# Scores of layer 0 in two rounded passes over stacked key halves, projections one PSUM bank at a time, joined latent weights

## The reference, cut to what matters

```python
qa, ka, va, f_logit, qb, kb, vb = jnp.split(h @ w_in, cuts, axis=-1)
# fox
s = jnp.einsum('bqhd,bkhd->bhqk', q, k) * (HEAD_DIM ** -0.5)
p = jax.nn.softmax(jnp.where(visible, s + decay, NEG_INF), axis=-1)
# stick-breaking
z = jnp.einsum('bqhd,bkhd->bhqk', q, k) * (HEAD_DIM ** -0.5)
later = lax.cumsum(log_rest, axis=-1, reverse=True) - log_rest
a = jnp.exp(log_beta + later)
# layer 1
z = h @ w_down                       # 384 + 256 + 32 columns
cq, ckv, kr = jnp.split(z, [Q_LORA, Q_LORA + KV_LORA], axis=-1)
```

## Time and profile before

| | |
|---|---|
| median of 3 runs | 1447.9 us (1446.54 to 1451.47) |
| the profiled execution's own time | 1455.13 us |
| its span, first to last instruction | 1453.4 us |
| PE, DVE, ACT busy | 1203.3, 655.4, 391.2 us |

### The profile page before, as it was taken

One profiled execution on the slowest core, in us unless ns is written; L12 is line 12 of the kernel. 1 busy time (PEld: TensorE's weight loads), 2 busy tenths in 40 slices (PEclk: granted clock), 3 DMA queues, 4 the chain that ended last, 5 costly groups with the idle time before them and its releaser, 6 DMA issues. The chain is left out here.

```text
span 1453.4 us, 23857 instructions
## 1 busy us (share of the span) xinstructions
PE 1203.3 (83%) x8148; PEld 833.9 (57%) x8148; DVE 655.4 (45%) x1819; ACT 391.2 (27%) x903; POOL 239.9 (17%) x366
## 2 busy tenths in 40 slices
PE   7999999987966997777497899999799499877760
PEld 5777777765854564344264676766587355444430
DVE  5455544446571542122362355555566445222227
ACT  4334444445111211011121244444521021111111
POOL 1222232220103232221110000000001222222113
PEclk9899999999977999999798999999899599989995
DMA  5222324206169999999620300000032999999965
GB/s 177 76 68 74 105 91 147 94 18 243 73 286 339 375 364 374 378 372 411 255 75 19 131 17 16 31 15 16 22 143 119 365 374 359 359 374 384 394 275 195
DMA packets 61407, 290.75 MB, mean 200 GB/s; under 512 B 12720, under 2 KB 23152, under 8 KB 44288
## 3 DMA queue, kind: packets, MB, share of 16 engines
q1 hardware_dynamic: 49440, 265.90, 49.5%
q0 software_dynamic: 10560, 18.90, 4.1%
q10 hardware_dynamic: 1312, 4.72, 0.8%
HBM read 275.91 MB, written 29.29 MB: 210 GB/s over the span
## 5 line engine op out<-in xcount | busy, mean ns | idle before, releaser
L1738 PE MATMUL psum<-w_gu,moe_xgT 128*64 128x256 f32 x1968 | 261.2, 410 | 71.1 <-DMA w_gu<-in_w_gate_up 56.1
L1738 PEld LDWEIGHTS psum<-w_gu,moe_xgT 128*64 128x64 f32 x1968 | 154.2, 146 | 162.3 <-issue 116.3
L199 PE MATMUL psum<-x_hi,ab_w_hi 128*128 128x288 f32 x384 | 126.6, 330 | 2.7 <-DVE ab_k_tok L877 1.6
L1811 DVE COPY moe_xgT<-psum 128x512 f32<-128x512 f32 x64 | 44.3, 692 | 166.0 <-PE psum L1728 165.1
L201 PE MATMUL psum<-x_hi,ab_w_lo 128*128 128x288 f32 x384 | 115.7, 301 | 0.0
L1685 POOL DMA_INDIRECT y_d<-mix,moe_slots x60 | 55.5, 926 | 364.0 <-DVE mix L1824 364.0
L200 PE MATMUL psum<-x_lo,ab_w_hi 128*128 128x288 f32 x384 | 115.6, 301 | 0.0
L1786 ACT ACTIVATE moe_silu<-psum 64x256 f32<-64x256 f32 x64 | 24.2, 378 | 338.9 <-PE psum L1738 293.8
L1755 PE MATMUL psum<-w_dn,moe_hidT 128*64 128x512 f32 x352 | 85.1, 604 | 2.2 <-issue 2.2
L1819 DVE COPY moe_hidT<-psum 128x128 f32<-128x128 f32 x64 | 18.7, 291 | 143.1 <-PE psum L1746 141.5
L199 PEld LDWEIGHTS psum<-x_hi,ab_w_hi 128*128 128x128 f32 x384 | 74.5, 194 | 9.5 <-issue 7.6
(11 more groups left out here) (305 smaller groups left out, 2124.0 us busy)
## 6 DMA issues: line engine op xcount, KB each, us to landing
w_gu<-in_w_gate_up SPq DMA_DIRECT2D x54, 2048.0 KB, 35.4
w_dn<-in_w_down SPq DMA_DIRECT2D x44, 1024.0 KB, 37.4
xT<-in_w_down SPq DMA_DIRECT2D x20, 1024.0 KB, 38.6
w_gu<-in_w_gate_up SPq DMA_DIRECT2D x10, 1536.0 KB, 40.5
w_gu<-in_w_out SPq DMA_DIRECT2D x4, 2048.0 KB, 7.9
combine_ys<-y_d SPq DMA_DIRECT2D x16, 512.0 KB, 8.5
xT<-in_w_gate_up SPq DMA_DIRECT2D x10, 512.0 KB, 41.8
xT<-cum_d SPq DMA_DIRECT2D x8, 544.0 KB, 6.6
```

Source lines behind the costliest of these rows:

```text
L199: nc.tensor.matmul(dst, r32(ah), r32(bh), start=first, stop=False)
L1738: last = nc.tensor.matmul(gu(s)[h * CB:(h + 1) * CB, 0:EH], xgT[:, s, j, :], gate_up_tile(k.w_gu[n], j)[:, h * EH:(h + 1) * EH], start=(j ...
L1811: nc.vector.tensor_copy(xgT[:, s, :, :].rearrange("p j q -> p (j q)"), xtr(s)).then_inc(xgT_ready, 1)
```

## The change

- Scores of layer 0: two fp32r passes in place of one fp32 product. `k_both` holds for each head the rounded keys on one half of the partitions and their low rest on the other; `q_hi` holds the rounded queries on both halves (the second by a copy), `q_lo` their rest on one half and zeros on the other. The first pass is q_hi by both halves of the keys, the second q_lo.
- The cached keys are loaded to a room of their own, `k_past_room`, and split behind units 0 (ACT) and 1 (DVE).
- Projections: step 0 is all input features into bank 6, step 1 all into bank 7; each bank's copies follow it. k's first step moves from behind unit 2 to behind unit 1. A pair's first scores no longer wait for its v; its first `values` does.
- The second buffers of q and k lie in the room of `w_gu[0]`, so half 0 of `w_out` is loaded behind the last scores of pair 7, and ACT and DVE wait for the gates' last readers before pair 0.
- `w_rope` becomes the last 32 columns of `w_latent`: two groups of matmuls (512 and 160 columns) in place of three.

```diff
-AB_AFTER = {"q0": -1, "q1": 0, "k0": 2, "k1": 3, "kt": 4, "v0": 5, "v1": 7, "vt": 8}
+AB_AFTER = {"q0": -1, "q1": 0, "k0": 1, "k1": 3, "kt": 4, "v0": 5, "v1": 7, "vt": 8}
...
-                        banks_free(p, 2 if n == 1 else 4)
+                        banks_free(p, 4 if n == 1 else 7)
...
-                    half = int(step[1])
-                    if half == 0:
-                        banks_free(p, (0, 1, 3)[n], (s[f"lo{n}"], p + 1))
-                    for j in range(4 * half, 4 * half + 4):
-                        for b in range(2):
...
+                    b = int(step[1])
+                    at = slice(b * HT, (b + 1) * HT)
+                    banks_free(p, (0, 1, 5)[n] + (b if n == 1 else 0), *([(s[f"lo{n}"], p + 1)] if b == 0 else []))
+                    for j in range(J):
...
+                        pieces = [(0, width, 0)] if t < 4 else [(0, PAST, PAST_AT), (PAST, width, SEQ)]
+                        for q, first in ((q_hi[par][h], True), (q_lo[par][h], False)):
+                            for a, b, at in pieces:
+                                last = nc.tensor.matmul(slot(u)[0:rows, a:b], r32(q[:, at_t]), r32(k_both[par][h][:, at:at + b - a]),
+                                                        start=first, stop=not first)
...
ACT
+                            copy(r32(hi[0][0:HD, at]), halves[0:HD, b, :], HD ** -0.5).then_inc(s["q_hi_done"], 1)
+                            return copy(r32(hi[1][HD:P, at]), halves[HD:P, b, :], HD ** -0.5)
...
+                    if step == "q1":
...
+                        copy(r32(hi[0][HD:P, :]), hi[0][0:HD, :])
+                        copy(r32(hi[1][0:HD, :]), hi[1][HD:P, :]).then_inc(s["q_twice"], 1)
+                    if step == "k1":
+                        hold(act, passed, (s["proj_dve"], n))
+                        copy(r32(k_both[par][0][0:HD, 0:T]), kT[0:HD, :]).then_inc(s["k_hi_done"], 1)
+                        copy(r32(k_both[par][1][HD:P, 0:T]), kT[HD:P, :]).then_inc(s["k_hi_done"], 1)
...
DVE
+                    if step == "k1":
+                        both = k_both[par]
+                        hold(dve, passed, (s["k_hi_done"], 2 * p + 1), (s["proj_dve"], n))
+                        split_lo(nc, both[0][HD:P, 0:T], kT[0:HD, :], both[0][0:HD, 0:T])
+                        hold(dve, passed, (s["k_hi_done"], 2 * p + 2))
+                        split_lo(nc, both[1][0:HD, 0:T], kT[HD:P, :], both[1][HD:P, 0:T]).then_inc(s["k_lo_done"], 1)
...
+                def split_past(p, par):
+                    hold(dve, passed, (s["kp_hi"], p + 1))
+                    both = k_both[par]
+                    split_lo(nc, both[0][HD:P, PAST_AT:], k_past[0:HD, :], both[0][0:HD, PAST_AT:])
+                    split_lo(nc, both[1][0:HD, PAST_AT:], k_past[HD:P, :], both[1][HD:P, PAST_AT:]).then_inc(s["kp_lo"], 1)
...
combine
-            for lo, hi, w in ((0, BANK, k.w_latent[:, :, 0:BANK]), (BANK, DOWN - ROPE, k.w_latent[:, :, BANK:]), (DOWN - ROPE, DOWN, k.w_rope)):
+            for lo, hi in ((0, BANK), (BANK, DOWN)):
```

More of the change, by code:

```diff
@@ L146, in __init__ @@
         self.xT = sb("xT", [P, J, TP])
-        self.mix = sb("mix", [P, NT, D])
+        mix_room = sb("mix", [P, J * DOWN])
+        self.mix = mix_room[:, 0:NT * D].rearrange("p (t d) -> p t d", t=NT)
         self.ident = sb("ident", [P, P])
@@ L151, in __init__ @@
         self.logits = sb("logits", [P, NT, GROUPS + NE])
-        self.w_latent = self.mix[:, :, :].rearrange("p t d -> p (t d)").rearrange("p (j n) -> p j n", j=J)
-        self.w_rope = sb("w_rope", [P, J, ROPE])
+        self.w_latent = mix_room[:].rearrange("p (j n) -> p j n", j=J)
         self.w_latent_in = ctx.enter_context(nc.semaphore("w_latent_in"))
@@ L163, in __init__ @@
         self.turn_of = sb("turn_of", [P, NE])
+        with ExitStack() as early:
+            lent = lambda n, w: early.enter_context(nc.sbuf_tensor(f"lent_{n}", [P, w], F32))[:, :]
+            self.lent_q = [lent(n, T) for n in ("q_hi0", "q_hi1", "q_lo0")]
+            self.lent_k = [lent(f"k_both{h}", KEYS) for h in range(2)]
         self.w_gu = [[sb(f"w_gu{s}", [P, J, 2 * EH])[:, :, :]] for s in range(2)]
@@ L258, in store @@
         sp.wait_ge(self.cum_ready, 2)
-        sp.dma_start(k.cum_d, self.cum).then_inc(self.out, 16)
+        sp.dma_start(k.cum_d, self.cum).then_inc(self.cum_out, 16)
         sp.wait_ge(self.tok_e, 4)
@@ L262, in store @@
         sp.dma_start(k.o_logf_s.rearrange("a b t h -> (a b t) h"), self.tok[0:NEW, 4, :]).then_inc(self.out, 16)
-        sp.wait_ge(self.out, 48)
+        sp.wait_ge(self.cum_out, 16)
+        sp.wait_ge(self.out, 32)
     def fill(self, pool):
@@ L431, in attend @@
         n_zeroed = 5 if mla else 8
-        STEPS = 6 if mla else 5
+        STEPS = 6 if mla else 8
         before_evened = 0 if mla else UNITS * SB_PAIRS
@@ L507, in store @@
                     at = p - SB_PAIRS if kind == "fox" else p
-                    done = STEPS * p + (5 if kv else 3)
+                    done = STEPS * p + (8 if kv else 5)
                     hold(sp, passed, (s["proj_act"], done), (s["proj_dve"], done))
@@ L628, in scores @@
                     elif u >= LEAD:
                         used = u - 3 + (u % 2) if u >= UNITS - 2 else u - 4
[L631 to L634, removed]
@@ L635, in scores @@
-                    if width > BANK:
-                        last = nc.tensor.matmul(slot(u)[0:rows, BANK:width], q, key[:, BANK:width], start=True, stop=True)
+                        hold(pe, passed, (s["scored"], n - u + used + 1), *([(s["kp_lo"], p + 1)] if u == UNITS - 2 and not mla else []))
+                    at_t = slice(t * P, t * P + rows)
+                    if mla:
+                        q, key = qh[par][h][0:QW, at_t], kh[par][h][0:QW, lo:lo + width]
+                        last = nc.tensor.matmul(slot(u)[0:rows, 0:min(width, BANK)], q, key[:, 0:min(width, BANK)], start=True, stop=True)
+                        if width > BANK:
+                            last = nc.tensor.matmul(slot(u)[0:rows, BANK:width], q, key[:, BANK:width], start=True, stop=True)
+                    else:
+                        pieces = [(0, width, 0)] if t < 4 else [(0, PAST, PAST_AT), (PAST, width, SEQ)]
[3 more added lines that the diff above has]
+                                                        start=first, stop=not first)
@@ L654, in values @@
                     n = NT * p + t
+                    if t == 0 and not mla:
+                        hold(pe, passed, (s["proj_act"], STEPS * (p + 1)), (s["proj_dve"], STEPS * (p + 1)))
                     hold(pe, passed, (s["probsT_used"], UNITS * p + 2 * t + 2), (s["o_done"], n), *([(s[f"vp_in{par}"], of_parity(16, p, par))] if t == 4 and not mla else []))
@@ L688, in _ @@
                 each_pair(pe, pair)
-            copied = list(MLA_AFTER) if mla else ["q1", "k1", "kt", "v1", "vt"]
+            copied = list(MLA_AFTER) if mla else list(AB_AFTER)
             after_of = MLA_AFTER if mla else AB_AFTER
@@ L803, in pair @@
                         copies(u)
+                        if u == 0 and not mla:
+                            split_past(p, par)
                         splits(split, p, par, u)
@@ L810, in _ @@
                 first_copies(split, copy_out, gates_part)
+                if not mla:
+                    hold(act, passed, (gates.cum_out, 16), (gates.tok_t, 1))
                 each_pair(act, pair)
@@ L962, in pair @@
                         copies(u)
+                        if u == 1 and not mla:
+                            split_past(p, par)
                         splits(split, p, par, u)
```

101 lines of the change are left out of this document (63 added, 38 removed).

## The result

The changed kernel takes 1463.96 us (median of 4 runs, 1462.56 to 1466.02), the kernel before 1448.51 in the same comparison (1446.54 to 1451.47): ratio 1.0106, 95% interval 1.0084 to 1.0128. It is slower by 15.4 us. The forecast was 1452.5 us, slower by 4.6. Its sign was right, but the loss is more than three times the forecast's: the time lies outside the 1448 to 1457 us of the likeliest case, and inside the 1436 to 1465 of all cases only by 1 us.

The account below looks back on a forecast made before the run. PE was taken to set the pace, with order-dependent waits between q and v. Sb pairs +5.6, fox pairs +2.1, clock +5, prologue and last pair -1.4, latents -6.7 sum to +4.6: 1452.5 us; likeliest 1448 to 1457, all cases 1436 to 1465.

Parts of the forecast that it names:

- the likeliest case: The forecast's own case: slower by 0 to +9 us, 1448 to 1457 us; chance 0.55.
- PE's work: Layer 0 scores: two rounded passes, 0.107 us each at 128 or fewer columns, cut PE's work by 2.8 us a pair.
- The chain to v: From q's end, new DVE and ACT copies delay v: 16.45 instead of 14.3 us in sb pairs, about 15.8 in fox.
- Unit 3's wait: Unit 3's transposes wait 1.6 us for unit 2's copy-out, which stands behind w_v's high part on ACT.
- Net: only -0.74 outside this stretch is left.: Of PE's 2.8 us, 0.74 is saved outside q to v; net +1.4 us per sb pair, +0.7 per fox pair.
- The clock: Half-rate falls in some two thirds of seven pairs, 1 us each: +5 us, bounds 0 and +12.
- The last pair: The pair without projections, its units following one another through three engines, gains 0.7 of its 2.8 us.
- The prologue: Before the first pair, k need not wait for both of q's copies: about -0.7 us.
- Latents and w_out: Joined latents' weights: four tiles at -1.5 and the last at -0.7, -6.7 us; later loading of w_out: 0, bound +2.
- Rival 2: Waits and clock both worse: a half-rate stretch in each pair and four-cycle narrow pieces, 1464 us; chance 0.2.
- narrow pieces: Rival 2's term for rounded score products on narrow pieces costing four cycles a column: +5 us.
- Rival 1: DVE and ACT hide the new copies: 1437 us, or 1418 if PE never waited; chance 0.25, hardly any at 1418.

Follow-up runs that it names:

- e11: The changed kernel with only the next w_k's split moved from behind unit 8 to the start of the next pair: 1456.84 us.
- e6: The changed kernel with the cached keys' splits and the next w_k's split both moved to the start of the pair: 1445.79 us.
- e7: The kernel before with the joined latents' weights and w_k's split moved to the start of the pair: 1429.50 us.
- e3: The changed kernel with one plain fp32 pass of the scores in place of two rounded ones, q's low rest left out: 1462.51 us.
- e8: The changed kernel with cached keys' and w_k's splits moved to the pair's start and the new keys' splits deferred to unit 5: 1431.03 us.
- e12: e8 with the fox pairs' cached keys split one pair ahead and w_v's split behind unit 2 in place of unit 1: 1420.81 us.
- e5: The changed kernel with only the cached keys' splits moved to the start of the pair, ahead of q's first copy: 1456.31 us.
- e2: The changed kernel with the four splits of the new keys put behind the copies for kt, at unit 5: 1466.71 us.

## Why the prediction was right in sign and too small

- **PE's work.** Right: the first rounded passes of 128 columns follow one another every 0.11 us (forecast 0.107), and the 81 ns of the Trainium skill, "TensorE: Matmul & The Clock Gate", "Back-to-back issue gap", did not come here:

```profile
88.99 0.27 PE L650 MATMUL psum<-lent_k_both,lent_q_lo 128*128 128x128 f32 x1
89.10 0.28 PE L650 MATMUL psum<-lent_k_both,lent_q_hi 128*128 128x128 f32 x1
```

- **The chain to v.** Right, and well sized: 16.8 against 16.45 in three sb pairs, and 16.4 against 15.8 in the one fox pair without a half-rate stretch on the way (267.6 to 284.0). Unit 3's wait, forecast at 1.6 us, was 1.25 and 0.58 ahead of unit 2's. Counted alike in both traces, v moved by 2.4 us in the sb pairs (14.45 before) and by 1.95 in that fox pair.
- **"Net: only -0.74 outside this stretch is left."** Wrong; this is the step that failed. From v to the end of the next q, before took 23.8 us, and after 23.5 and 23.6 in the two fox pairs whose clock held there: -0.2 to -0.3. In the sb pairs after has no such stretch at full clock (24.7 with a fall in it), so the figure is carried over to them. PE's savings there ran into the stall at the pair's end (2.02 us against 1.89 before), which e11, e6 and e7 show to be w_k's split on ACT and DVE. With the chain it makes +2.1 a pair in four sb pairs and +1.8 in three fox pairs, +13.8 us in place of the forecast's +7.7.
- **The clock.** The mechanism was right and the size roughly: some +8 us in place of +5, within its bounds of 0 and 12. The 8 is a remainder (below) and was not measured by itself; e3, which has no fall in the sb pairs, ends the attention 6.8 us earlier, with 22 us more work for PE and 3.1 us of waits for w_q in it. The place was forecast as v: two falls of the seven pairs stand there, three in k's second bank, and the others at the pairs' starts. Over the attention, 15 to 365 us, the granted clock was 0.92, and 0.96 before. The rule of the Trainium skill, "TensorE: Matmul & The Clock Gate", section "What's actually happening", that activity holds the clock, agrees with e3 (1.00 with more work, 0.93 with less).
- **The last pair.** Wrong: +1.8 us from its first scores to the end (340.62 to 365.17 against 318.52 to 341.27) in place of -0.7. The forecast took units as flowing through three engines; DVE had 1.78 us more between two `logits`, and the clock fell to 0.70. The prologue was +0.5 in place of -0.7.
- **Latents and w_out.** -6.9 against -6.7, but a tile gave 1.31 us and not 1.5; up to 1 us of the sum may be the clock's, which was at half rate for 7.6 us of that stretch before and for 5.1 after. w_out +0: no engine waits for its halves in the trace.
- **What was missing.** The wait of SP's queue for `kp_lo`. The forecast looked at ACT, DVE and PE, and not at what is queued behind the cached keys' load. It cost the changed kernel 0.5 us only, but left no slack for mending it.

The attention's 23.9 us less 13.8, 1.8 and 0.5 (prologue) leave 7.8 for the clock, so the sum is no test of it. The places fit: the fourth sb pair, with the two falls from 188.7 and 198.9, is 3.4 us longer than the other three (44.9 against 41.5), and the last fox pair is another 3 us longer than its chain explains (33.0 us from q's end to the last pair's first scores, 28.2 before). The 15.4 us of the medians against the 10.9 of the profiled executions comes from the executions: that of before was 6.6 us above its median, that of after 2.1.

Of the signs named in advance, v at 16 to 17 us behind DVE's copy of k_tok, unit 3's wait and the latents came; the copies of q lie 41.5 to 44.9 us apart and not 39 to 41, and half-rate stretches at v came in two pairs.

Rival 2 (waits and clock both worse, 1464 us) named the time by luck: its +5 for narrow pieces did not come, its +12 for the clock was some 8, and what filled the gap, the stall at a pair's end and the last pair, it did not have. Rival 1's 1437 us needed an order that hides the new copies; e8 and e12 are that order, and their times lie below it because they mend the old stall as well.

Open: how much of e5's gain is ACT's work and how much DVE's. Also whether the bank-by-bank projections gain by themselves.

## What to carry to other kernels

When work moves from the engine that sets the pace to others, ask in which idle stretch of theirs it will stand, not what their share of busy time is: in one order the change, without its latents, cost 23 us; with its copies and w_k's split moved it was level with the old kernel mended alike (e8, e7) or 8.7 us faster (e12), and the cheap places were where those engines wait for the first result of a stage. A fix can measure zero because a second wait behind it takes the gain; e2 gave +2.7 us alone and -14.8 behind two moves, so test fixes together before dropping one. And a room that is filled by DMA and freed later than before delays every load behind it in the same queue.

## What the runs showed of the hardware

A rounded pass of 256 columns follows the last after 0.12 us where one of 128 takes 0.11 (e8, timeline of a pair's first scores), and one of 288 columns 0.134: 2.25 times the width costs 1.2 times the time.

```profile
117.48 0.28 PE L650 MATMUL psum<-ab_k_both,ab_q_lo 128*128 128x256 f32 x1
117.60 0.28 PE L650 MATMUL psum<-ab_k_both,ab_q_hi 128*128 128x256 f32 x1
```

And giving PE more to do, 22 us in all, left the time where it was (e3): the granted clock of the sb pairs rose from 0.93 to 1.00.
